# Attention on one core: the row halves of the sums' bank by head instead of by key block, and transposes in place of a fold

## The reference

```python
# group A, 8 heads: dense, chunk-causal
s = (einsum('bqhd,bshd->bhqs', q_nope, k_nope) + einsum('bqhd,bsd->bhqs', q_rope, k_rope)) * scale
p = softmax(where(mask, s, -inf))
o_a = einsum('bhqs,bshd->bqhd', p, v)
# group B, 8 heads on 2 key heads: the same on the 256 keys that an indexer scores highest
s = where(valid, einsum('bqjgd,bqnjd->bqjgn', q, k_gathered) * dh ** -0.5, -inf)
o_b = einsum('bqjgn,bqnjd->bqjgd', softmax(s), v_gathered)
```

## Time and profile before

| | us |
|---|---|
| time before, median of 3 runs | 4021.95 (4019.14 to 4025.28) |
| the profiled execution, first to last instruction | 4030.5 |
| PE busy over that span | 3675.7 (91%) |
| DVE busy | 2164.7 (54%) |
| ACT busy | 1674.0 (42%) |
| POOL busy | 1382.2 (34%) |

### The profile page before, as it was taken

One profiled execution on the slowest core, in us unless ns is written; L12 is line 12 of the kernel. 1 busy time (PEld: TensorE's weight loads), 2 busy tenths in 40 slices (PEclk: granted clock), 3 DMA queues, 4 the chain that ended last, 5 costly groups with the idle time before them and its releaser, 6 DMA issues. The chain is left out here.

```text
span 4030.5 us, 57699 instructions
## 1 busy us (share of the span) xinstructions
PE 3675.7 (91%) x20367; PEld 2824.8 (70%) x20367; DVE 2164.7 (54%) x4098; ACT 1674.0 (42%) x3126; POOL 1382.2 (34%) x894
## 2 busy tenths in 40 slices
PE   7999978787888888899888898999999999999998
PEld 6777744555565555666566776888788788889986
DVE  4222237499998889999994433441344044224411
ACT  4333322455666666676655222331332133223311
POOL 0000010455565555665300001444444444443332
PEclk9999989689999999999999999999999999999999
DMA  4232231201000000000000654334434243433321
GB/s 166 80 90 88 77 94 46 53 28 34 27 21 21 21 21 17 18 10 18 11 16 23 229 205 149 94 100 145 119 94 144 96 122 95 156 110 94 83 105 59
DMA packets 325589, 320.24 MB, mean 79 GB/s; under 512 B 44576, under 2 KB 261424, under 8 KB 325344
## 3 DMA queue, kind: packets, MB, share of 16 engines
q1 hardware_dynamic: 310576, 265.30, 22.3%
q0 software_dynamic: 7488, 25.87, 1.8%
q10 hardware_dynamic: 7344, 26.74, 1.6%
HBM read 247.66 MB, written 70.19 MB: 79 GB/s over the span
## 5 line engine op out<-in xcount | busy, mean ns | idle before, releaser
L1948 DVE TENSOR_SCALAR_CACHE_REDUCE at_hit<-at_score,at_su 128x384 bf16<-128x384 f32 (+13 forms) x406 | 599.6, 1477 | 5.1
L1394 DVE TENSOR_TENSOR ff_a_lo<-ff_prod,ff_a_hi 128x512 f32 (+1 forms) x110 | 410.7, 3734 | 170.8 <-ACT ff_a_hi L1346 170.8
L1249 POOL TENSOR_TENSOR fh_w_lo<-fh_stage,fh_w_hi 128x2048 fp32r<-128x2048 f32 x67 | 309.2, 4615 | 463.6 <-ACT fh_w_hi L1332 463.6
L1680 PE MATMUL at_p_t<-at_ident,at_prob 128*128 128x128 f32 x2176 | 334.6, 290 | 145.5 <-ACT at_prob L1760 144.7
L1249 POOL TENSOR_TENSOR ff_w_lo<-fh_stage,ff_w_hi 128x2048 fp32r<-128x2048 f32 (+1 forms) x68 | 296.2, 4356 | 431.8 <-ACT ff_w_hi L1332 412.8
L1760 ACT ACTIVATE at_prob<-at_prob,at_st 128x1024 f32<-128x1024 f32 (+7 forms) x384 | 342.9, 896 | 170.1 <-DVE at_st L1917 169.8
L1680 PEld LDWEIGHTS at_p_t<-at_ident,at_prob 128*128 128x128 f32 x2176 | 250.7, 145 | 226.1 <-ACT at_prob L1760 195.1
L1857 POOL TENSOR_TENSOR at_rel<-at_rel,at_iws 128x512 f32<-128x512 f32 (+3 forms) x304 | 284.0, 934 | 340.3 <-ACT at_rel L1782 262.9
L1775 ACT ACTIVATE at_probt<-at_p_t 128x512 f32<-128x512 f32 (+3 forms) x640 | 313.9, 533 | 165.9 <-PE at_p_t L1680 162.5
L1342 ACT ACTIVATE ff_prod<-ff_bank 128x512 f32<-128x512 f32 (+1 forms) x110 | 57.0, 518 | 646.2 <-PE ff_bank L97 646.1
L95 PE MATMUL ff_bank<-fh_h_hi,fh_w_hi 128*128 128x512 f32 (+1 forms) x880 | 309.8, 352 | 10.5 <-DVEq L1381 6.9
(11 more groups left out here) (313 smaller groups left out, 8052.2 us busy)
## 6 DMA issues: line engine op xcount, KB each, us to landing
fh_stage<-in_w_gate SPq DMA_DIRECT2D x86, 512.0 KB, 3.9
fh_stage<-in_w_up SPq DMA_DIRECT2D x86, 512.0 KB, 5.1
fh_stage<-in_w_down SPq DMA_DIRECT2D x40, 1024.0 KB, 5.1
pj_xt<-in_xT SPq DMA_DIRECT2D x17, 512.0 KB, 3.4
pj_x<-in_x SPq DMA_DIRECT2D x17, 512.0 KB, 4.2
mx_o<-scr_o SPq DMA_DIRECT2D x17, 512.0 KB, 7.1
mx_x<-in_x SPq DMA_DIRECT2D x17, 512.0 KB, 3.6
scr_x<-mx_x ACTq DMA_DIRECT2D x17, 512.0 KB, 8.0
```

What stands on the lines that cost most here:

```text
L1249: pool.tensor_tensor(w_lo[a][:, 0:w], stage[a][:, 0:w], w_hi[a][:, 0:w].bitcast(F32), ALU.subtract).then_inc(s_wlo, 1)
L1394: dve.tensor_tensor(a_lo[:, ds(2 * q + a, 1), to], prod[b][:, 0:gr.Nh].unsqueeze(1), a_hi[:, ds(2 * q + a, 1), to].bitcast(F32), ALU.subtr ...
L1680: mm = pe.transpose(p_t[t_turn.at(n, f) % 2][:, b * P:(b + 1) * P], prob[h % 2][:, a + b * P:a + (b + 1) * P], ident[:, :])
L1948: step(dve.tensor_scalar(h_, s_, cand.bitcast(F32), 0.0, ALU.is_ge, ALU.add, cnt))
```

## The change

The halves of `p_o` now hold two heads: all key blocks of an even head sum into rows 0 to 63, all blocks of the odd head after it into rows 64 to 127. ACT copies the bank once per pair of heads, 128 rows by 128 columns, into `mixed`. At the end of a half tile PE transposes the four pairs back, each 128 by 128, which yields 128 queries by two heads of 64; there is nothing to add. The constant `fold` and its two transfers are gone. An even head's first `add_values` waits for the copy of the pair before; an odd head's waits for none.

```diff
-                if u == 0:
-                    t_half.wait(pe, n, h)
+                if u == 0 and h % 2 == 0:
+                    t_pair.wait(pe, n, h // 2)
                     t_oev.wait(pe, n, h // HA)
...
-                    side = blk % 2 * VA
+                    side = h % 2 * VA
                     mm = pe.matmul(p_o[side:side + VA, 0:P], vals, probt[t_turn.at(n, f) % 2][:, b, :],
-                                   start=blk < 2, stop=blk + 2 >= t.blocks)
+                                   start=blk == 0, stop=blk == t.blocks - 1)
...
-            def fold_halves(n, g):
-                t_half.wait(pe, n, (g + 1) * HA)
-                rows = min(2, tiles[n].blocks) * VA
-                for k in range(HA):
-                    mm = pe.matmul(p_o[:, k * VA:(k + 1) * VA], halves[0:rows, k, :], fold[0:rows, :], start=True, stop=True)
-                mm.then_inc(t_fold.sem, 1)
+            def turn_back(n, g):
+                t_pair.wait(pe, n, (g + 1) * HA // 2)
+                for k in range(HA // 2):
+                    mm = pe.transpose(p_o[:, k * P:(k + 1) * P], mixed[:, k, :], ident[:, :])
+                mm.then_inc(t_back.sem, 1)
...
-            def take_halves(n, h):
+            def take_pair(n, h):
                 t_pv.wait(act, n, (h + 1) * tiles[n].U)
-                t_fold.wait(act, n, h // HA)
-                rows = min(2, tiles[n].blocks) * VA
-                act.activation(halves[0:rows, h % HA, :], p_o[0:rows, 0:P], ACT.Copy).then_inc(t_half.sem, 1)
+                t_back.wait(act, n, h // HA)
+                act.activation(mixed[:, h % HA // 2, :], p_o[:, 0:P], ACT.Copy).then_inc(t_pair.sem, 1)
...
-                if s:
-                    take_halves(*slots[s - 1])
+                if s and h % 2 == 0:
+                    take_pair(*slots[s - 1])
```

More of the change, by code:

```diff
@@ L1542, in attend_prompt @@
         out = m.sb("out", [P, 512])
-        halves = m.sb("halves", [P, HA, P])
-        ident, fold = m.sb("ident", [P, P]), m.sb("fold", [P, VA])
+        mixed = m.sb("mixed", [P, HA // 2, P])
+        ident = m.sb("ident", [P, P])
         st = m.sb("st", [P, 72])
@@ L1565, in attend_prompt @@
         t_turn, t_pt, t_pv = (tally(x, lambda t: H * t.U) for x in ("probs_turned", "turned_taken", "values_added"))
-        t_half = tally("halves_taken", lambda t: H)
+        t_pair = tally("pair_taken", lambda t: H // 2)
         t_ask, t_told = (tally(x, lambda t: len(HELPED) if t.searched else 0) for x in ("candidate_set", "signs_summed"))
         t_inv = tally("sums_inverted", lambda t: 2)
-        t_fold, t_oev, t_norm = (tally(x, lambda t: 2) for x in ("halves_folded", "values_taken", "out_normed"))
+        t_back, t_oev, t_norm = (tally(x, lambda t: 2) for x in ("pairs_turned_back", "values_taken", "out_normed"))
         t_ifill, t_relu, t_wtd, t_acc = (tally(x, lambda t: HI * t.U if t.searched else 0)
@@ L1625, in _ @@
             sp.dma_start(ident[:, :], io["ident"]).then_inc(s_const, 16)
-            for half in range(2):
-                sp.dma_start(fold[half * VA:(half + 1) * VA, :], io["ident"][0:VA, 0:VA]).then_inc(s_const, 16)
             sp.dma_start(prob[1][:, 0:P], io["causal_bias"][:, SEQ:SEQ + P]).then_inc(s_const, 16)
@@ L1718, in index_unit @@
                 stacked(p_i[:, 0:w], qi_hi[:, h, :], qi_lo[:, h, :], kv["KB"][:, NKV, a:a + w]).then_inc(t_ifill.sem, 1)
-            pe.wait_ge(s_const, 64)
+            pe.wait_ge(s_const, 32)
             product(0, 0, 0)
@@ L1735, in _ @@
                 if h % HA == 0 and s:
-                    fold_halves((s - 1) // H, (s - 1) % H // HA)
+                    turn_back((s - 1) // H, (s - 1) % H // HA)
                 for q in index_units(s, 1):
@@ L1748, in _ @@
                 add_values(*slots[-1], u)
-            fold_halves(TP - 1, 1)
+            turn_back(TP - 1, 1)
         @block.scalar
@@ L1790, in sparse_queries @@
                 act.activation(qb_hi[:, :, :], qb_lo[:, :, :].bitcast(F32), ACT.Copy).then_inc(t_qbhi.sem, 1)
-            def take_halves(n, h):
+            def take_pair(n, h):
                 t_pv.wait(act, n, (h + 1) * tiles[n].U)
-                t_fold.wait(act, n, h // HA)
-                rows = min(2, tiles[n].blocks) * VA
-                act.activation(halves[0:rows, h % HA, :], p_o[0:rows, 0:P], ACT.Copy).then_inc(t_half.sem, 1)
+                t_back.wait(act, n, h // HA)
+                act.activation(mixed[:, h % HA // 2, :], p_o[:, 0:P], ACT.Copy).then_inc(t_pair.sem, 1)
             def take_values(n, g):
-                t_fold.wait(act, n, g + 1)
+                t_back.wait(act, n, g + 1)
                 if 2 * n + g:
@@ L1828, in _ @@
                     exps(*nxt)
-            take_halves(*slots[-1])
+            take_pair(*slots[-1])
             take_values(TP - 1, 1)
@@ L1871, in _ @@
             pool.memset(tail[:, 0:TAIL - P], 0.0).then_inc(s_zero, 1)
-            pool.wait_ge(s_const, 64)
+            pool.wait_ge(s_const, 32)
             pool.tensor_copy(tail[:, TAIL - P:TAIL], prob[1][:, 0:P]).then_inc(s_zero, 1)
@@ L2028, in _ @@
             plans = {t.n: search(t) for t in tiles if t.searched}
-            dve.wait_ge(s_const, 64)
+            dve.wait_ge(s_const, 32)
             dve.wait_ge(s_zero, 2)
```

## The result

The changed kernel takes 4059.63 us in the median (4 runs, 4052.12 to 4060.41) against 4022.6 for the kernel before, measured beside it: a ratio of 1.0086, 95% interval 1.0071 to 1.0100. It is 37 us slower by the medians, 35 by the ratio. The direction and the range (4045 to 4170) hold; the size does not, since +78 was forecast.

A forecast was written before the change was run, and what follows sets the result against it. DVE and PE were taken as nearly full together in tiles 4 to 14, PE alone bounding tile 15. Terms of -6, +4, +20, +41, +26 and -7 gave +78, so 4100 us, range 4045 to 4170.

The forecast's parts named there:

- The pairing: Value products of the prompt's attention: each of 1024 pairs of blocks costs 0.218 us more on PE, 223 us in sum.
- The fold, the copies, the start: Half tile ends: transposes save 1.3 us each, more in tile 0; 128 copies fewer on ACT, nothing; earlier bias, -1.0 us.
- the forecast's last rival: Value products: neighbours of one head overlap anyway, only savings are left, some -18 us, 4004 us; chance 0.03.
- Tiles 0 to 3: First stretch of the prompt's attention: tile 0 gains, other added work stays inside PE's idle time; -6 us.
- Weights in the open: Rival on value products: 4096 records each grow by a 55 ns weight load, 225 us more, about 4320 us; chance 0.03.
- halves that do not matter: Value products: the halves are not what pairs the records, so the added 223 us vanish, 4004 us; chance 0.03.
- Tile 15: Last tile of the prompt's attention, PE already the bound: 134.2 us against 108.0, +26 us.
- Tiles 4 to 7: Second stretch: PE stays under DVE's 299.9 us, a tenth of the added 41.9 us gets through; +4 us.
- Tiles 8 to 14: Third and fourth stretches: PE becomes the bound at 96% busy; +20 and +41 us, before the clock's -7.
- the forecast's own sign: Its size is wrong if tiles 4 to 11 grow by over 60 us or by nothing.
- The clock: PE in tiles 8 to 14: the lower clock level withholds 43 us; fewer gaps give back a sixth, -7 us.
- The first rival: Prompt's attention: PE fills all its waits and regains the clock, 4022 to 4045 us; chance 0.08.

The follow-up runs named there:

- last tile alone: The kernel before, with all key blocks summed into rows 0 to 63 in tile 15 only: 4051.0 us, 1.0066.
- the change with pairs: The changed kernel with blocks alternating between the halves again, copies per pair of heads and four transposes kept, part of the computation missing: 3997.12 us, 0.9939.
- the useless products: The kernel before, with two f32 products of no use ahead of each head's first transposes: 4027.07 us; in tiles 8 to 14 alone, four 4021.98, one 4012.78.
- one half for all blocks: The kernel before, with all key blocks of every head summed into rows 0 to 63, copy per head and fold kept: 4095.52 us, 1.0182.

## Why the prediction was right or wrong

- **The pairing: right.** Bursts of 0.65 and 1.96 us were forecast and measured; the two groups of value products in tiles 8 to 14 went from 211.9 (106.5 + 105.4) to 344.6 us (174.1 + 170.5), +133 for +140, and in the whole stage they take 568 us for some 580. Without cover a pair costs 0.20 to 0.21 us (last tile alone) for 0.218.
- **The fold, the copies, the start: put too low.** With pairs kept, the forecast's last rival puts all the savings at 18 us; the change with pairs saves 27. That rival halves the 18 us of folds in tiles 8 to 14, but with pairs these tiles became 13 to 17 us shorter, and less clock is withheld in them. Tiles 0 to 3 gained 7.1 for 6, which decides little: the same code takes 201 to 211 us there in the profiles of other runs. The start gave next to nothing: PE's wait for the bias is 8.82 us instead of 9.01, for -1.0.
- **Weights in the open, halves that do not matter:** both rivals fell; the bursts show the pace of a lone block and nothing beside it. The rule of the Trainium skill's page *TensorE: Matmul & The Clock Gate* (Part 3, The mechanism), that a weight load overlaps a running matmul only when the row groups differ, does not agree with the trace: eight blocks on one half, all on the same 128 rows, take 1.96 us, with no load in the open.
- **Tile 15: right.** 131.8 us at 98% of PE, for 134 at 97%.
- **Tiles 4 to 7:** -0.1 for +4, by profiles that cannot tell these apart: the kernel before's own code takes 315 to 320 us there in single executions.
- **Tiles 8 to 14: here it failed.** Forecast +20 + 41 - 7 = +54, measured 862.1 against 852.5, +9.6. PE's share was well put: 831.7 of 862.1 us is 96.5% for the 96% assumed. But its work was 831.7 us, not 459.2 + 417.8 = 877.0. Of the 45 us missing, some 33 are work that the change does not touch: all but value products and folds took 511.7 us before (755.6 - 211.9 - 32.0) and 478.7 after (831.7 - 344.6 - 8.4). Another 7 are value products and 5 folds that came out cheaper than forecast. The busy times of groups overlap at their ends, so these parts are estimates; with each moment counted for the record that started last they are 31, 9 and 5. By the forecast's own sign, tiles 4 to 11 growing by nothing (they shrank by 2.2), it is wrong in its size.

The step that failed is the term "**The clock** ... I take a sixth, -7". What the clock withheld in tiles 8 to 14, 43 us by the forecast's own reading, came back nearly whole: by PEclk 0.95 to 0.99 and 1.00, that is 0.04 x 456 + 0.05 x 406 = 38 us. With the whole of it in place of a sixth the sum is 78 - 36 = +42, against 37 by the medians and 27 by the two profiles; tiles 8 to 14 come to +18, against 10 to 14. By the trace's clock records PE was at work for 82 of the 85 us for which the clock stood at its lower level in these tiles before, and for 10 us after: at half the pace that is 36 of the 45 us. The other 9 stay open.

What the change did to bring the clock back is in part open. That work in the waits is enough is what the useless products show: they leave fold, copies and pairs as they were, and 0.98 to 1.00 comes back. That nothing else in the change did it is not shown: with the fold and half of the copies gone, but the pairs kept and the waits longer than before, some 12 to 17 us came back too (the change with pairs), and with a fold and waits as short as in the changed kernel 14 us stayed withheld (one half for all blocks).

The first rival, all waits filled and the clock regained, was priced at 4022 to 4045. Its clock came true; its filling did not: 30 us of PE's 97 idle us in tiles 8 to 14 remained. That 4060 lies inside the forecast's range is in part luck: its low end, 4045, supposes all waits filled and 18 us of clock back.

## What to carry to other kernels

Products that fill half of the rows of a bank should alternate halves between neighbours: here the second was free, 0.44 us for two blocks against 0.43 for one, and an arrangement that saved folds and copies but broke that lost more than it saved. When work is added to PE beside another full engine, read the granted clock of the stretch first: what it withholds can be credit for the added work, here 38 of 43 us. Where PE only waits, a little useless work in the wait can pay for itself, here 12 us.

## What the runs showed of the hardware that was not expected

In tiles 8 to 14 the kernel before let PE wait up to 2.9 us at a time for exponentials and got 0.95 of the clock; the changed kernel waits for them up to 1.0 us there and got 0.99 and 1.00. (Its longest wait for anything there is 1.8 us, for ACT's `at_rel`.) The waits of tiles 8 to 14, before first:

```profile
PE at_p_t L1680 <- ACT at_prob L1760: 65.3, 60, 2.9
```

```profile
PE at_p_t L1678 <- ACT at_prob L1757: 9.2, 19, 1.0
```

With one useless product per head, 112 in all, the clock was 0.98 and 0.99, though waits up to 2.5 us remained:

```profile
PE at_p_t L1684 <- ACT at_prob L1764: 44.5, 50, 2.5
```

So neither the sum of the waits nor the longest one tells the clock by itself: the change with pairs waits up to 2.9 us as well, and longer in sum, and got 0.96 and 0.98. The fold may have a part in it: in the run with one half for all blocks, whose folds take 64 rows, six of the nine falls of the clock in tiles 8 to 15 come right behind a fold of 2.00 us, with no wait over 0.8 us beside it. That the fold caused them is not shown.

Fillers made of f32 transposes and of f32 products brought nearly the same clock, 0.98 and 0.99 against 0.99 and 1.00.
